# Where the selection of prompt tiles 4 to 7 stands in a hybrid decoder layer's order of work: beside the samples' attention or beside the first feed-forward group

## The reference

```
q, k, v, qi, ki, wi, u = rope / split of rmsnorm(x) @ w_in          # one projection
score  = sum over 4 index heads of relu(qi . ki) * wi               # indexer
idx    = top_k(score masked to the past, 256)                       # selection, per query
a_o    = softmax(q . k[idx]) @ v[idx]                               # 8 heads, 2 kv heads, width 64
s_o    = GLU of a diagonal complex state-space scan over u
x      = x + rmsnorm([a_o, s_o] @ w_out)
x      = x + rmsnorm(square(relu(rmsnorm(x) @ w_up)) @ w_down)      # 1024 -> 4096 -> 1024
```

## Time and profile before

| | us |
|---|---|
| median of 3 runs | 3765.61 |
| lowest and highest run | 3762.29, 3767.79 |
| span of the profiled execution | 3765.1 |
| TensorE, VectorE, ScalarE, GpSimd busy | 3068.1, 2160.7, 1845.4, 1286.6 |

### The profile page before, as it was taken

One profiled execution on the slowest core, in us unless ns is written; L12 is line 12 of the kernel. 1 busy time (PEld: TensorE's weight loads), 2 busy tenths in 40 slices (PEclk: granted clock), 3 DMA queues, 4 the chain that ended last, 5 costly groups with the idle time before them and its releaser, 6 DMA issues.

```text
span 3765.1 us, 47305 instructions
## 1 busy us (share of the span) xinstructions
PE 3068.1 (81%) x15388; PEld 2414.3 (64%) x15388; DVE 2160.7 (57%) x4196; ACT 1845.4 (49%) x3065; POOL 1286.6 (34%) x1134
## 2 busy tenths in 40 slices
PE   7997535537778889997788999868888999789997
PEld 6886421214556668765577886546677888678885
DVE  4433952973356984467897443777995443643333
ACT  3322413722446755575674556756754554433333
POOL 1333510313013561252265114522663112235454
PEclk9998767767779999998899999989999999989998
DMA  4444344527332232123223112242222111522222
GB/s 153 141 138 166 64 153 108 135 68 222 99 113 76 81 94 68 55 78 136 97 77 95 54 43 63 81 148 69 72 90 83 54 40 50 177 81 87 79 79 76
DMA packets 201425, 361.56 MB, mean 96 GB/s; under 512 B 56202, under 2 KB 113612, under 8 KB 199740
## 3 DMA queue, kind: packets, MB, share of 16 engines
q1 hardware_dynamic: 182652, 332.01, 27.9%
q0 software_dynamic: 9312, 18.14, 1.5%
q10 hardware_dynamic: 9216, 8.39, 0.7%
HBM read 298.64 MB, written 67.01 MB: 97 GB/s over the span
## 4 chain that ended last, share of the span: by engine, by line
PE 42%; DVE 18%; issue 12%; ACT 5%; POOL 4%; DMA 2%; SPq 1%; ACTq 1%; POOLq 0%; DVEq 0%
PE r L1532 11%; PE r L1564 9%; PE po L1612 4%; PE r L1505 3%; PE tr L1603 3%; DVE junk_v_b L2242 3%; POOL acc_b L2008 2%; ACT junk_a_b L1873 2%; DVE trial_b L2194 2%; DVE up_b L2089 2%; DVE dn_b L2089 2%; PE sc L1580 1%; PE sc L1591 1%; PE sc L1590 1%; PE r L1675 1%
## 5 line engine op out<-in xcount | busy, mean ns | idle before, releaser
L1564 PE MATMUL r<-dn_b,h_b 128*128 128x512 f32 x2880 | 727.0, 408 | 111.8 <-DVE dn_b L2089 51.2
L1564 PEld LDWEIGHTS r<-dn_b,h_b 128*128 128x128 f32 x2880 | 551.4, 196 | 273.1 <-DVE dn_b L2089 61.7
L2008 POOL TENSOR_TENSOR acc_b<-acc_b,part_b 128x512 f32<-128x512 f32 x375 | 527.8, 1427 | 517.2 <-ACT part_b L1824 516.3
L1532 PE MATMUL r<-x_hi_b,up_b 128*128 128x512 f32 x2048 | 660.2, 396 | 7.6 <-DVE x_lo_b L2108 4.2
L1532 PEld LDWEIGHTS r<-x_hi_b,up_b 128*128 128x128 f32 x2048 | 389.2, 190 | 105.5 <-issue 13.0
L1873 ACT ACTIVATE junk_a_b<-score_b,trial_b 128x384 int8<-128x384 f32 (+13 forms) x266 | 347.4, 1306 | 148.5 <-DVE trial_b L2194 147.8
L1989 POOL TENSOR_TENSOR hr_b<-hr_b 128x512 f32<-128x512 f32 x128 | 153.5, 1199 | 738.4 <-ACT hr_b L1811 738.1
L1532 PE MATMUL r<-x_lo_b,up_b 128*128 128x512 f32 x1024 | 402.7, 393 | 0.0
L1824 ACT ACTIVATE part_b<-r 128x512 f32<-128x512 f32 x390 | 223.9, 594 | 225.0 <-PE r L1564 156.0
L1612 PEld LDWEIGHTS po<-V_sb,pT_b 128*128 128x128 f32 x2176 | 291.5, 195 | 23.2 <-issue 3.1
L1900 ACT ACTIVATE pT_b<-tr 128x512 f32<-128x512 f32 (+3 forms) x320 | 169.0, 528 | 259.5 <-PE tr L1603 257.8
(11 more groups left out here) (385 smaller groups left out, 5696.3 us busy)
## 6 DMA issues: line engine op xcount, KB each, us to landing
raw_b<-w_up SPq DMA_DIRECT2D x128, 512.0 KB, 3.8
raw_b<-w_down SPq DMA_DIRECT2D x128, 512.0 KB, 3.5
raw_b<-w_out SPq DMA_DIRECT2D x64, 256.0 KB, 3.2
kv_b<-kv_pages SPq DMA_DIRECT2D x96, 128.0 KB, 4.0
kv_b<-kv_pages POOLq DMA_DIRECT2D x96, 128.0 KB, 3.8
x_tok_sb<-x_all SPq DMA_DIRECT2D x17, 512.0 KB, 4.5
xT_sb<-xT_all SPq DMA_DIRECT2D x17, 512.0 KB, 4.8
kic<-kidx_d SPq DMA_DIRECT2D x4, 2048.0 KB, 8.5
```

The costliest lines, as they stand in the source:

```text
L1532: mm = pe.matmul(x[:], wt[:, c], y[:, k], start=k == n == 0, stop=(k, n) == (KD - 1, 2))
L1564: mm = pe.matmul(x[:], f[:, tok], w[:, col], start=c == n == 0, stop=(c, n) == (KQ - 1, 2))
L2008: pool.tensor_tensor(dst, dst, part[:, add_no[key] % 2, :], ALU.add).then_inc(add_pool, 1)
```

## The change

The samples' list is cut at its first `SS` unit. The part ahead of it (index scores, search) is merged with the selection of tiles 2 and 3. The part behind it (the attention of the samples) is merged, as the side list, with the attention of tiles 0 to 3 followed by the selection of tiles 4 to 7. The side list of groups 0 to 2 loses that selection and begins with the attention of tiles 4 to 7. No unit's own instructions change.

```diff
--- before.py
+++ after.py
@@ -866,12 +866,13 @@
                 i += 1
         return out + [u for u, _ in side[i:]]
 
-    samples, first_side = sample_units(), select_units(0) + attend_units(0)
+    samples, first_side = sample_units(), select_units(0)
+    found = next(i for i, (u, _) in enumerate(samples) if u[0] == "SS")
     plan = [u for u, _ in first_side[:2]] + [("SQ",)] + [u for u, _ in first_side[2:14]]
-    for u in merge(first_side[14:], samples[1:]):
+    for u in merge(first_side[14:], samples[1:found]):
         plan += [u] + [("GL", u[1] - 1)] * (u[0] == "SF" and 1 <= u[1] <= N_GATE)
-    plan += [("B",)]
-    late = [u for s in range(1, 4) for u in select_units(s) + attend_units(s)]
+    plan += merge(attend_units(0) + select_units(1), samples[found:]) + [("B",)]
+    late = attend_units(1) + [u for s in range(2, 4) for u in select_units(s) + attend_units(s)]
     plan += merge([u for g in range(NG - 1) for u in feed_units(g)], late)
     ended = []
     plan += [u for u, _ in ended + feed_units(NG - 1)] + [("Z",)]
```

## The result

The changed kernel takes 3787.3 us (median of 5 runs) against 3767.8 of the kernel before: the ratio is 1.0047, with a 95% interval of 1.0035 to 1.0060. It is slower, as forecast, but by 20 us and not by 53; the range held it. One of its runs, 3954 us, was disturbed and is left out of the ratio. The profiled execution has a span of 3788.0 us against 3765.1, so 22.9 us are to be found in the traces. A length in one profile is good to some us only: groups 0 to 2, whose list of units is the same in seven of the kernels profiled here, take 2058.2 to 2066.9 us in them.

A forecast was written before the change was run, and what follows sets the result against it. TensorE bounds the kernel, held up beside selection by loaded engines, while VectorE has room beside the samples' attention. Terms 16 + 117 - 80 = +53 on 3765.1 gave 3818 us; 8 in 10 range 3748 to 3882.

The forecast's parts named there:

- Term 1: Samples' search stretch: longer by 16 us, bounds 5 and 20, from 17 selection steps that must now end there.
- Term 2: Samples' attention stretch: longer by 117 us, 330 against 213, from the moved selection of tiles 4 to 7.
- walk: Samples' attention stretch: times summed piece by piece in the new list's order, 337 us, taken as 330 for overlap.
- Term 3: Feed-forward of groups 0 to 2: shorter by 80 us, bounds 45 and 130, as selection leaves and thins.
- Index matmuls: Feed-forward of groups 0 to 2: 64 index matmuls of tiles 4 to 7 leave, -12 us, bounds 8 and 30.
- The clock: First group's feed-forward beside selection: granted clock of 0.95 with 241 us busy, a gain of 10 us.
- TensorE's idle time: Groups 0 to 2: -26 us beside the departed selection, -20 from thinner selection, -12 in the first group's out-projection.
- The least for term 2: Samples' attention stretch: lower bound of 235 us (+22), VectorE's work alone at the 95% of the search.
- the fast rival: Samples' stretch: selection fits with VectorE at 90% or more, ending at 240 us; kernel 3709 us (-57), chance 0.16.
- The rival with little gain in the feed-forward: Feed-forward: gives back only 35 us, its idle time being its own; kernel 3863 us (+98), chance 0.16.
- the one in series: Samples' stretch: both chains nearly in series, page loads too, 390 us (+177); kernel 3878 us (+113), chance 0.10.
- The rule that spoke against the change: Samples' stretch: VectorE's 2-port instructions would delay GpSimd's page loads; the prediction took nothing for it.

The follow-up runs named there:

- Run 8: Changed kernel with tile 3's last 17 selection steps put back beside the samples' first pair of scores: 3772.3 us, ratio 1.0015 to the kernel before.
- Run 1: Changed kernel with the side units left in groups 0 to 2 kept at their old spacing, places of moved selection empty: 3811.8 us, ratio 1.0111.
- run 11: Changed kernel, tile 3's last 17 steps back beside the samples, only 45 of 104 steps of tiles 4 to 7 moved: 3760.1 us, ratio 0.9982.

## Why the prediction came out as it did

**The sign and the picture held, and the size did not.** VectorE's idle time beside the samples was not free room, and the three terms had the right signs. The forecast of +53 became +23 in the profile: the terms were off by +7, -10 and -28 us (and 1 us lies between them). The last one is the step that failed.

**Term 1, +16.** Measured 22.7, above its upper bound of 20. Run 8 shows the same 22. The 17 steps were counted at 17 us of VectorE, and beside the samples that is right: run 8 adds 212.5 - 195.2 = 17.3 us there. In the search the same steps are 184.8 - 162.6 = 22.2 us of VectorE, which is the whole 22.7. Of the 5 us between the two, 3 us are in the small second turns (L2195): ten more of them take 4.6 us in the search, and eleven 1.8 us beside the samples. So the price of this instruction, which the prediction took out of term 2, came back in term 1, where it wasn't looked for.

**Term 2, +117.** Measured 107.3, but the small error is in part luck. Piece by piece, with the end of each pair's output (L2375) and the start of its exponential (L1941) as bounds:

| | walk | measured |
|---|---|---|
| attention of tiles 0 to 3, first pair | 107 | 120.5 |
| scores of the second pair | 29 | 29 |
| values of the second pair | 43 | 36.5 |
| scores of the third pair | 42 | 42.5 |
| values of the third pair | 43 | 35 |
| scores of the fourth pair | 38 | 27.5 |
| values of the fourth pair | 35 | 31.5 |

The opening took 13.5 us more than given, and the rest 28 less. The value steps were given 3.4 us, as if a count and the issue of pages always added up; the intervals were 2.5 us in the mean, and taking the pages away gave 14 us, not 30. The third pair's scores met the number, but not for the reason given: in their first 22 us it was TensorE at 0.50 that was full, and not VectorE, and the walk had nothing for TensorE's clock. The last pair was at VectorE's pace, as the walk had it. VectorE's moved work was 195.2 - 72.4 + 17 = 140 us against the estimate of 150. The expected 158 ns of a small turn was 19.78/124 = 160:

```profile
916.00:1152.00 236.00, 19.78 (x124) 0.70 0.34 108
1595.00:1814.00 219.00, 32.06 (x69) 0.96 0.27 87
```

The second row is the selection of tiles 8 to 11 in the changed kernel, line L2195 alone: 465 ns, more than the 381 of the earlier trace rows. The rule of the Trainium skill, SBUF — State Buffer, section "SBUF: two separate sides", agrees with both rows; the page limits it to GpSimd instructions that read SBUF, as its additions do. But it did not make the total cheaper: beside the feed-forward the moved work was 189 us of VectorE by the rows of the kernel before, 49 over the 140, and VectorE's total there fell by only 1402.7 - 1262.3 = 140. With GpSimd's work the same (781 and 779 us), the price was passed to instructions that stayed: the low halves of weights (dn_b from 132.2 to 137.0 us, up_b from 156.5 to 160.2), the score sums and the small turns grew, all of which read two tensors in SBUF, while the remaining 104 counts, which read one, kept their 194.6 us. Run 1 bears it out. There GpSimd has 50 us less to do, and VectorE's total falls by 162, though it has 31 more sums of 0.69 us: by 184 if these are left out.

**Term 3, -80: the step that failed.** It measured 108.3, inside its bounds. The mechanism was right and the sizes of two of its parts were not. They can be told from the two kernels' rows, without run 1:

- Index matmuls: 12 forecast, 24.2 measured. I priced the half that lay in one window (32 of 64, 15.0 us), and took 12 for all. By their line they take 129.1 us in groups 0 to 2 before and 104.9 after.

```profile
1040.00:3215.00 2175.00, 129.09 (x288) 49.54 (x288) 0.94 0.25 80
```

```profile
1170.00:3237.00 2067.00, 104.89 (x224) 39.08 (x224) 0.95 0.26 83
```

- The clock: 10 forecast, 20.6 measured. TensorE's busy time fell by 44.8 us, of which 24.2 are index matmuls; the rest came back without a matmul less, at a mean clock of 0.95 in place of 0.94. Most of that, 13.6 us, is in the down-projections (604.4 to 590.8), which are the matmuls that had waited for VectorE.
- TensorE's idle time: 26 + 20 + 12 = 58 forecast, 63.5 measured.

These are 12.2, 10.6 and 5.5 us, the whole 28.3. So the term failed at two small sizes that were taken at half, the first because its row covered half of the instructions. Run 1 parts the same 108.3 by cause: thinning 21.8 against 20, and removal 86.5 against 60, as far as its 31 other sums leave that clear.

**Two slips of the sums.** The least for term 2 is (165 + 55) / 0.95 = 232, not 235. And the fast rival takes 100 us for the feed-forward, where the forecast's own term has 80, without a reason: with 80 it would be 3729 in place of 3709.

**The rivals.** The fast one needed a stretch under 277 us. It did not come: VectorE was busy for 61% of the stretch and not for 90%. That the chain across ScalarE and VectorE is the reason is likely, and not shown by itself, since TensorE and the page loads hold parts of the stretch too. Of the rule behind it, in the Trainium skill's Perfetto Trace Analysis, section "Optimization Strategy", that regimes with different contended engines may gain from interleaving: run 11 gains 6.5 us from a part of it, the whole loses 6 (run 8) or, with tile 3's steps in the search, 20. The rival with little gain in the feed-forward is refuted by 108 us, the one in series by 322. The rule that spoke against the change, VectorE holding up GpSimd's page loads, had no effect that can be seen: the issues take 538 ns in the median, with VectorE busy for 61% of the stretch. Two of them took over 600 ns (746 at most), which by its letter was named as a sign of being wrong; TensorE waited for no page. Whether the moved instructions run in the mode that the rule names, the trace doesn't tell.

```profile
L1242 POOL DMA_DIRECT2D kv_b<-kv_pages x96: 538/538/746, 620.3 to 1092.5; - x96
```

Of the signs named ahead, the first output projection of group 0 came at 1170.3, where 1170 was named, group 3 was unchanged, and TensorE was busy for 153.4 of 162 us (94.7%) beside the attention of tiles 4 to 7. The prediction named over 95% for it. VectorE's share after the attention of tiles 0 to 3 was 164.7 of 236 us, 69.8%, where over 70% was named. The small turns came at 160 ns. Counts 3 us and more apart beside value steps, the last sign, were 4 of 22.

## What to carry to other kernels

An engine's idle time in a stretch says how much work it could hold, not what the work costs: here the work was a chain across two engines and the stretch another chain across the same two, and with VectorE and ScalarE each busy for a third of it before, each us added to either after the move cost about 0.7. Measure the price of a us in both places, by doubling a harmless instruction, before moving work between them, and look at all engines on the path, the granted clock included. A move need not be all or nothing: here 45 of 104 steps gained 6.5 us where all of them lost 6. And what must make room ahead of the moved work counts too: more than half of the 20 us came from 17 steps pushed into a stretch where VectorE was full. When one prices a removal, count all of its instructions by line over the whole stretch, not those that fall into one window.

## What was not expected of the hardware

- ScalarE's sequencer can issue a transfer while the engine's last activation still runs (997.62, inside 996.82 to 997.76), so two page loads and a count need not add up: 2.0 to 3.5 us and 2.5 in the mean over 22 intervals.
- A VectorE instruction on 128x1 elements with two SBUF inputs takes 160 ns where GpSimd issues transfers, and 381 to 465 ns in the mean beside GpSimd's additions. Moving 189 us of selection away lowered VectorE's busy time there by only 140 us while GpSimd's work stayed, since other instructions with two SBUF inputs grew.
- Group 3 is 549 to 551 us long in eleven of the profiles and 546 in the three kernels without page loads on ScalarE, though none of its own instructions differ. No run tells why.
